# Routing from un-normalised x1 in a decoder layer with a sparse expert stage

## What is computed

```python
h  = rms_norm(x, norm1_g) * (1.0 + scale1) + shift1        # shift, scale, gate from silu(c) @ w_ada
x1 = x + gate1 * mixer(h, ...)                             # conv branch, differential attention, w_o
h2 = rms_norm(x1, norm2_g) * (1.0 + scale2) + shift2
logits = h2 @ w_router + b_router                          # 32 experts
top_vals, top_idx = top_k(logits, 4); wts = softmax(top_vals)
combine = sum(one_hot(top_idx) * wts[..., None], axis=1)
for e in range(32):
    gu  = h2 @ w_up[e] + b_up[e]                           # 1024 -> 2048
    glu = minimum(gu[:, 0::2], 7); lin = clip(gu[:, 1::2], -7, 7)
    act = glu * sigmoid(1.702 * glu) * (lin + 1.0)
    y  += combine[:, e:e+1] * (act @ w_down[e] + b_down[e])
out = x1 + gate2 * y
```

## Time and profile before

| | us |
|---|---|
| median of 3 runs | 1326.64 (1326.07 to 1327.2) |
| profiled execution, whole | 1327.75 |
| its span, first to last instruction | 1326.0 |
| PE busy | 1132.5 (85%) |
| DVE busy | 377.9 (28%) |
| ACT busy | 231.6 (17%) |
| POOL busy | 57.3 (4%) |
| DMA, mean over the span | 360 GB/s |
| mean granted TensorE clock | 0.934 of full |

### The profile page before, as it was taken

The page is one execution under the profiler, slowest core; times in us unless marked ns, Lnnn a source line. Parts: engine busy times, 40 slices in busy tenths (PEclk is TensorE's granted clock), DMA queues, the critical chain, the costliest instruction groups (busy, mean ns, idle before and its releaser), DMA issues.

```text
span 1326.0 us, 18358 instructions
## 1 busy us (share of the span) xinstructions
PE 1132.5 (85%) x7535; PEld 435.1 (33%) x7535; DVE 377.9 (28%) x1043; ACT 231.6 (17%) x448; POOL 57.3 (4%) x76
## 2 busy tenths in 40 slices
PE   3899999999979866667999776987869796999996
PEld 1684345444443211112333221322213231333331
DVE  1599946651251111100222110211101120212221
ACT  1200104450112011000122111111101121111220
POOL 2120000037000000000000000000000000000000
PEclk8899999999989788888999878998889898999998
DMA  8969393266579999999999999999999999599997
GB/s 315 332 237 379 127 378 129 92 175 224 200 267 387 424 426 428 426 425 426 426 424 424 425 426 426 424 426 426 425 425 424 426 427 426 235 409 423 421 425 316
DMA packets 69254, 477.57 MB, mean 360 GB/s; under 512 B 6744, under 2 KB 14969, under 8 KB 33358
## 3 DMA queue, kind: packets, MB, share of 16 engines
q1 hardware_dynamic: 66716, 472.66, 87.2%
q0 software_dynamic: 1200, 3.28, 1.0%
q10 hardware_dynamic: 1282, 0.80, 0.2%
HBM read 473.58 MB, written 1.05 MB: 358 GB/s over the span
## 4 chain that ended last, share of the span: by engine, by line
PE 47%; DMA 23%; SPq 18%; DVE 8%; ACT 3%; issue 1%; DVEq 0%
DMA weights<-in_w_down 18%; SPq L430 16%; PE bank L1372 15%; PE bank L1131 8%; PE bank L1399 8%; DVE weights L809 6%; PE bank L1347 4%; DMA weights<-in_w_up 3%; PE bank L1207 2%; PE bank L1266 2%; PE bank L1334 2%; PE bank L1354 1%; PE bank L1121 1%; PE bank L1340 1%; SPq L399 1%; DMA weights<-in_w_in 1%
## 5 line engine op out<-in xcount | busy, mean ns | idle before, releaser
L1372 PE MATMUL bank<-weights,buf_d 128*32 128x512 f32 x3008 | 393.6, 669 | 132.1 <-DMA weights<-in_w_up 132.1
L1372 PEld LDWEIGHTS bank<-weights,buf_d 128*32 128x32 f32 x3008 | 97.3, 117 | 404.1 <-DMA weights<-in_w_up 200.9
L1399 PE MATMUL bank<-weights,buf_d 128*32 128x512 f32 x1504 | 174.5, 597 | 10.0 <-DMA weights<-in_w_down 10.0
L1059 DVE TENSOR_SCALAR u_conv<-bank 128x256 f32<-128x256 f32 x47 | 20.0, 425 | 460.9 <-PE bank L1372 460.9
L690 ACT ACTIVATE u_conv<-u_conv 128x256 f32<-128x256 f32 x47 | 19.6, 416 | 642.6 <-DVE u_conv L1059 642.6
L1347 PE MATMUL bank<-buf_d 64*128 64x512 f32 x384 | 99.6, 638 | 0.9 <-DVE buf_d L1069 0.9
L809 DVE SCALAR_TENSOR_TENSOR weights<-u_conv,weights 128x256 f32<-128x256 f32 x240 | 99.3, 490 | 0.3
L1069 DVE TENSOR_TENSOR buf_d<-bank,u_conv 128x512 f32<-128x512 f32 x47 | 32.5, 692 | 224.9 <-PE bank L1399 224.9
L1131 PE MATMUL bank<-weights,buf_d 128*128 128x512 f32 x192 | 84.9, 604 | 2.3 <-DVE buf_c L842 2.3
L1399 PEld LDWEIGHTS bank<-weights,buf_d 128*32 128x32 f32 x1504 | 42.5, 109 | 106.7 <-issue 81.4
L1334 PE MATMUL bank<-buf_c,u_conv 128*32 128x256 f32 x768 | 60.4, 387 | 1.1 <-DVE u_conv L1028 1.1
(11 more groups left out here) (261 smaller groups left out, 764.3 us busy)
## 6 DMA issues: line engine op xcount, KB each, us to landing
weights<-in_w_up SPq DMA_DIRECT2D x128, 2048.0 KB, 33.7
weights<-in_w_down SPq DMA_DIRECT2D x64, 2048.0 KB, 37.2
weights<-in_w_ada SPq DMA_DIRECT2D x12, 2048.0 KB, 17.2
weights<-in_w_in SPq DMA_DIRECT2D x10, 2048.0 KB, 12.1
weights<-in_w_in SPq DMA_DIRECT2D x8, 1024.0 KB, 11.8
weights<-in_w_conv_out SPq DMA_DIRECT2D x2, 2048.0 KB, 11.7
weights<-in_w_attn_out SPq DMA_DIRECT2D x2, 2048.0 KB, 8.7
weights<-in_w_o SPq DMA_DIRECT2D x2, 2048.0 KB, 11.1
```

Of the source, the lines that this page charges most:

```text
L1372: ins = t.matmul(UP[SLOTS * g:SLOTS * g + SLOTS, :], xgT[:, r, SLOTS * j:SLOTS * j + SLOTS], w[:, r, NB * g:NB * g + NB], start=False, sto ...
L1399: ins = t.matmul(DOWN[rows, :], actT[:, r, at:at + SLOTS], w[:, g, r, NB * i:NB * i + NB], start=(r == 1 and h == 0 and g == 0), stop=(h = ...
```

## The change

- **Router.** h2 is not made for all tokens any more. The un-normalised x1 is transposed; the router's rows are multiplied beforehand by (1 + scale2) * norm2_g (`wr`), and shift2's part is summed into one row `b2`. The logits come out transposed in four partition groups, are folded by `esum`, and multiplied by each token's 1/rms (`rstd2`) in one step with b2. Both tiles go through top-k together.
- **mod2.** The modulation of the second norm is held as columns: two new PSUM uses ("mod2T") on PE behind the V projection. The 16 POOL transfers that spread modulation rows become 12, for gate1 and gate2.
- **First unit.** All tokens of expert 0's first unit are found from expert 0's rank alone (`pos0`), gathered and transposed before the unit table exists. `routed`, `upper`, `tri`, ranks and the table's base are bf16.
- **Gather.** Units gather raw x1 with rstd2 in `pick`. After the transposition DVE applies scale and shift per column (`apply_mod`). ACT's copy of 512 columns becomes one of 256 (Cmb). pickw's transposes go to bank TR, ahead of act's.
- **Slots.** x_tok has its own buffer. SLOT_ORDER is new; SP's waits on the gate copies and the h2 transposes go, a wait on POOL's bias rows (`ebias_ready`) ahead of chunk 3 is new. POOL starts these rows when the last head's scores are done, with buffers in HEAD_SLOT.
- **Start.** The small loads (lambda, q/k gains, positions; gate and conv-out biases, router, b_ada rows) move from SP's queue to ACT's: eight behind the h1T activations, twelve behind the third GLU sigmoid. The rope and lambda work on DVE moves from ahead of glu_tile(0) to behind glu_tile(2), with ACT's Sin and Exp behind the third sigmoid. The conv taps are loaded as 248 rows of 128 and transposed in two steps.

The diff, cut to its core:

```diff
-GATE_SLOT, VALUE_SLOT, HEAD_SLOT, X_SLOT, SMALL_SLOT = 6, 7, 8, 9, 10
-SLOT_ORDER = (0, VALUE_SLOT, 1, 2, 3, GATE_SLOT, 4, 5, HEAD_SLOT, X_SLOT, SMALL_SLOT)
+GATE_SLOT, VALUE_SLOT, HEAD_SLOT, CONV_SLOT, SMALL_SLOT = 6, 7, 8, 9, 10
+SLOT_ORDER = (0, VALUE_SLOT, 1, HEAD_SLOT, 2, 3, CONV_SLOT, GATE_SLOT, 4, 5, SMALL_SLOT)
...
-        order += [("h2T", 0), ("h2T", 1), ("logits", 0), ("h2T", 2), ("h2T", 3), ("logits", 1)]
-        order += [(name, 0) for name in ("totals", "counts", "ends", "routing", "units")]
+        order += [("x1T", i) for i in range(4)]
+        order += [(name, 0) for name in ("lgT", "logits", "rank", "gather", "ends", "combT", "units")]
...
@@ SP: block loads @@
-                if n == CONV0:
-                    for i, w in enumerate((lambda_q1, lambda_k1, lambda_q2, lambda_k2)):
-                        sp.dma_start(lam_in[:, i, :], w.to_broadcast([P, HD])).then_inc(in_small, 16)
...
@@ SP: expert chunks @@
             load_chunk(0, 2)
+            sp.wait_ge(ebias_ready, 3 * PARTS)
+            load_chunk(0, 3)
             for i in range(2):
                 sp.wait_ge(*used[AOUT0 + i])
-                load_chunk(0, 3 + i)
+                load_chunk(0, 4 + i)
+            full(sp, YA_USE + 3)
+            load_chunk(1, 0)
             full(sp, MT_USE + 3)
-            load_chunk(0, 5)
+            load_chunk(1, 1)
             for i in range(2):
                 sp.wait_ge(*used[WO0 + i])
-                load_chunk(1, i)
-            sp.wait_ge(gate2_ready, 2)
-            load_chunk(1, 2)
-            full(sp, H2T_USE[3])
-            load_chunk(1, 3)
+                load_chunk(1, 2 + i)
             sp.wait_ge(units_ready, 2)
             load_chunk(1, 4)
...
@@ ACT: behind h1T @@
+            for i, w in enumerate((lambda_q1, lambda_k1, lambda_q2, lambda_k2)):
+                load(lam_in[:, i, :], w.to_broadcast([P, HD]), in_small)
...
+            for k in range(3):
+                glu_gate(k)
+            for q in range(3):
+                load(bias_f[32 * q:32 * q + 4, :], b_gate[0].rearrange("(i n) -> i n", n=NB), in_rowsb)
...
@@ ACT: routing @@
+            for i in range(3):
+                square(i // 2, i % 2)
+            for i in range(3):
+                keep_x1T(i)
+            square(1, 1)
+            act_e.wait_ge(h_rms, 1)
+            act_e.wait_ge(h_sq, 4)
+            for tt in range(TT):
+                s.activation(rstd2[:, tt:tt + 1], h_ss[:, 1, tt:tt + 1], ACT.Sqrt, scale=1.0 / D,
+                             bias=h_bias[:, tt:tt + 1]).then_inc(h_rms, 1)
+            full(act_e, LGT_USE)
+            s.copy(lgT_sb, bank(LGT_USE)[:, 0:T]).then_inc(bank_free[LGT_USE % 4], 1)
...
@@ ACT: unit loop @@
                 s.copy(actT, TR[:, 0:T].rearrange("p (r s) -> p r s", r=2)).then_inc(actT_ready, 1)
-                act_e.wait_ge(xt_done, u + 2)
-                s.copy(area_q[:, 0:2 * T], GX[:, :]).then_inc(xc_ready, 1)
+                s.copy(Cmb, TR[:, T:2 * T]).then_inc(cmb_ready, 1)
...
@@ DVE: x1 @@
+            def add_branch(tt, half):
...
+                step(v.tensor_tensor(bank(use)[:, :], bank(use)[:, :], gate1[:, cs], ALU.mult))
+                v.tensor_tensor(x_tok[:, tt, cs], x_tok[:, tt, cs], bank(use)[:, :], ALU.add).then_inc(bank_free[use % 4], 1)
...
@@ DVE: routing @@
+            v.tensor_scalar(pos0[:], bank(RK_USE)[:, T + 4:T + 4 + TT], -ROUTED, None, ALU.add).then_inc(pos0_ready, 1)
+            step(v.tensor_copy(ecol[0:EXPERTS, 0:1], bank(RK_USE)[0:EXPERTS, T:T + 1]))
+            dve.wait_ge(pos0_ready, 1)
+            for tt in range(TT):
+                ins = v.tensor_scalar(pick[:, tt, :], place_s[:, 0, :], pos0[:, tt:tt + 1], rstd2[:, tt:tt + 1],
+                                      ALU.is_equal, ALU.mult)
+            ins.then_inc(pick_ready, 1)
...
+            step(v.tensor_scalar(above[:], thr[:], ecol[e, 0:1], None, ALU.is_lt))
+            step(v.tensor_reduce(ecol[e, 1:2], above[:], axis=AX, op=ALU.add))
+            v.tensor_copy(m_col[:, 0:1], ecol[e, 1:2]).then_inc(m_ready, 1)
...
+            def apply_mod(link, at, done):
+                seen = GX[:, T:2 * T].rearrange("p (r g s) -> p r g s", r=2, g=GROUPS)
+                to = xgT.rearrange("p r (g s) -> p r g s", g=GROUPS)
+                link(v.tensor_tensor(to, seen, xg_scale.unsqueeze(3).to_broadcast([P, 2, GROUPS, SLOTS]), ALU.mult), at)
+                v.tensor_tensor(to, to, xg_shift.unsqueeze(3).to_broadcast([P, 2, GROUPS, SLOTS]), ALU.add).then_inc(done, 1)
...
@@ PE: unit @@
                 gather()
+                pe.wait_ge(pickw_ready, u + 1)
+                for tt in range(TT):
+                    t.transpose(TR[:, T + P * tt:T + P * tt + P], pickw[:, tt, :], ident[:])
                 pe.wait_ge(act_ready, u + 1)
                 transpose_halves(TR, 0, act).then_inc(t_done, 1)
                 pe.wait_ge(xs_ready, u + 2)
-                transpose_halves(GX, T, xg)
-                pe.wait_ge(pickw_ready, u + 1)
-                for tt in range(TT):
-                    ins = t.transpose(GX[:, P * tt:P * tt + P], pickw[:, tt, :], ident[:])
-                ins.then_inc(xt_done, 1)
+                transpose_halves(GX, T, xg).then_inc(xt_done, 1)
```

More of the change, by code:

```diff
@@ L340, in build @@
         WO_USE = use_of["w_o", 0]
-        H2T_USE = [use_of["h2T", i] for i in range(4)]
-        LG_USE = [use_of["logits", i] for i in range(TT)]
-        RT_USE = use_of["routing", 0]
-        TOT_USE = use_of["totals", 0]
-        CNT_USE = use_of["counts", 0]
-        END_USE = use_of["ends", 0]
-        UN_USE = use_of["units", 0]
+        M2T_USE = [use_of["mod2T", i] for i in range(2)]
+        X1T_USE = [use_of["x1T", i] for i in range(4)]
+        LGT_USE, LG_USE, RK_USE, GA_USE, END_USE, CT_USE, UN_USE = (
+            use_of[n, 0] for n in ("lgT", "logits", "rank", "gather", "ends", "combT", "units"))
+        assert GA_USE % 4 == 1
         MEAN_USE, VAR_USE = use_of["mean", 0], use_of["var", 0]
@@ L675, in _, with square @@
-            act_e.wait_ge(lg_ready, 1)
-            s.activation(tw[:], topf[:], ACT.Exp).then_inc(tw_ready, 1)
-            full(act_e, RT_USE)
-            s.copy(routedT[:], bank(RT_USE)[0:EXPERTS, 0:T])
-            s.copy(combT[:], bank(RT_USE)[0:EXPERTS, T:2 * T]).then_inc(bank_free[RT_USE % 4], 1)
+            def square(tt, half):
+                freed(act_e, WO_USE + 2 * tt + half)
+                if tt or half:
+                    act_e.wait_ge(h_sq, 2 * tt + half)
+                s.activation(junk, x_tok[:, tt, NB * half:NB * half + NB], ACT.Square,
+                             accum_out=h_ss[:, half, tt:tt + 1]).then_inc(h_sq, 1)
@@ new lines, in _ @@
+            for i in range(3):
+                add_branch(i // 2, i % 2)
+            dve.wait_ge(h_sq, 3)
+            v.tensor_scalar(h_bias[:], h_ss[:, 0, :], 1.0 / D, EPS, ALU.mult, ALU.add).then_inc(h_rms, 1)
+            step(v.tensor_copy(area_k[:, 2128:2128 + KD], mod2[:, 1, :]))
+            step(v.tensor_copy(area_k[:, 2128 + KD:2128 + 2 * KD], mod2[:, 0, :]))
+            add_branch(1, 1)
+            full(dve, X1T_USE[3])
+            v.tensor_copy(x1T[:, 4:8, P:2 * P], bank(X1T_USE[3])[:, :].rearrange("p (k t) -> p k t", k=4)).then_inc(
+                bank_free[X1T_USE[3] % 4], 1)
@@ L1003, in _ @@
+            ins.then_inc(comb_ready, 1)
             full(dve, END_USE)
@@ new lines, in turn_x1, with seed @@
+            def turn_x1(i):
+                use, tt, half = X1T_USE[i], i // 2, i % 2
+                fill(pe, use)
+                for j in range(4):
+                    kk, r = 2 * half + j // 2, j % 2
+                    ins = t.transpose(bank(use)[:, P * j:P * j + P],
+                                      x_tok[:, tt, T * kk:T * kk + T].rearrange("p (c r) -> p r c", r=2)[:, r, :], ident[:])
+                ins.then_inc(bank_full[use % 4], 1)
+            def seed(tt, i):
+                t.matmul(Y[tt][i][:, :], ident[:], x_tok[:, tt, NB * i:NB * i + NB], start=True, stop=True, skip_group_check=True)
@@ new lines, in _ @@
+            for i in range(4):
+                turn_x1(i)
+            seed(0, 0)
+            fill(pe, LGT_USE)
+            for i in range(4):
+                freed(pe, X1T_USE[i])
+            pe.wait_ge(ws_ready, 2)
+            for r in range(2):
+                for g in range(GROUPS):
+                    ins = t.matmul(bank(LGT_USE)[EXPERTS * g:EXPERTS * g + EXPERTS, 0:T], wr[:, 2 * g + r, :], x1T[:, 2 * g + r, :],
+                                   start=(r == 0), stop=(r == 1))
+            ins.then_inc(bank_full[LGT_USE % 4], 1)
@@ L1293, in _ @@
+            seed(1, 0)
+            seed(1, 1)
             pe.wait_ge(routed_ready, 1)
-            fill(pe, TOT_USE)
+            b = bank(RK_USE)
+            for j in range(TT):
+                for tt in range(j + 1):
+                    t.matmul(b[:, T + 4 + j:T + 5 + j], upper[:, tt, P * j:P * j + P], routed[:, tt, 0:1], start=(tt == 0), stop=(tt == j))
```

(1 more changed line is left out.)

500 lines of the change are left out of this document (265 added, 235 removed).

## The result

The changed kernel takes 1314.28 us in the median of four runs (1313.38 to 1315.13), the ratio to the kernel before is 0.9907 (95% interval 0.9887 to 0.9926): 12.4 us faster. The profiled execution took 1313.38, its span is 1311.6 (before 1326.0). L numbers are lines of the changed kernel from here on; in the experiments they are shifted, mostly by a few, in start_as_before by up to 35 (its L868 is L833).

What follows compares the result with a forecast made beforehand. The prediction took a chain of PE and DVE, then routing, then the expert weight stream at DMA rate as the bound. Its terms, -10.9 + 3.5 + 1.7 - 1.2 = -6.9, gave 1319.7 us by the median, range 1314 to 1327.

Steps and rivals of the forecast that it cites:

- the main case: Whole kernel: the summed forecast of 1319.7 us, own range 1317 to 1323, chance 0.56.
- The terms (a) that place the end: Expert weight stream: it starts for good after its first chunk is used, so shifting the first expert matmul shifts the end.
- The routing, forecast -10.9: From last W_o matmul to first expert matmul: 27.1 us before, first expert matmul at 388.8, a gain of 10.9 us.
- The ScalarE drain: ACT's table change in the routing: a possible 1.38 us drain besides the 1.28 us load, left out of the sum.
- The start, forecast -2.2: Before the first conv matmul: small loads on ACT's queue let w_in come sooner, h1T at 38.7 is next late, -2.2 us.
- The rope and lambda block, forecast +6.2: DVE work moved behind glu_tile(2), onto a path without slack: 5.0 us own work plus ACT's answer, +6.2 us.
- the upstream cost is hidden: Rival: POOL's work meets rope instead of the taps, the early half clock costs less; upstream +1.7, 1316.2 us, chance 0.17.
- Upstream together, forecast +5.2: Everything before the routing: start and rope taken as +3.5 us, plus 1.7 for mod2's transposes, a loss of 5.2.
- mod2's columns: PE between V projection and QK's transposes: two uses of four f32 transposes cost +1.7 us (1 to 2).
- Cover for chunks 7 to 9: Weight chunks before the expert stage: they wait for less and are there by 381, which is cover, not gain.
- The unit loop, forecast -1.2: Expert units: pickw's transposes going first save 0.2 us per unit, -1.2 us together (0 to -2).
- The slower rival: Rival at the start: ACT's small-load issues stall and delay sigmoid, taps and rope's Sin; +8, 1335 us, chance 0.12.

Runs made afterwards that it cites:

- start_as_before: Changed kernel with small loads, rope and lambda work, and ACT's Sin and Exp put back at their earlier places, keeping the new conv-taps form: 1314.21 us.
- delay: Changed kernel with six extra 128x512 f32 matmuls on PE between the unit table and the first unit: 1319.23 us.
- chunks_late: Changed kernel with SP holding weight chunks 7 to 9 until the routing logits are on PE: 1319.93 us.
- best1: Changed kernel with rope and lambda between the first two glu_tiles, POOL's bias operations held until seven QK tiles are done, and PE's loop-bound read earlier: 1305.70 us.
- conv_rows_old: Changed kernel with the conv taps again loaded as one transfer of 31 rows of 4 KB and turned by eight transposes: 1319.08 us.
- small_on_sp: Changed kernel with the eight small loads issued again on SP's queue ahead of w_in: 1321.41 us.
- pool_late: Changed kernel with POOL's five bias operations held until QK's second tile is done, behind 142 us: 1311.73 us.
- after_again: The changed kernel run once more without any edit: 1314.34 us.

## Why the prediction was right, and where it was wrong

**How right.** The direction and the size of the routing's gain were right. The total was not: the main case gave itself 1317 to 1323, and 1314.28 lies below it, near the lower end that came from a case held at 0.17. In the profiled executions the change is -14.4 us where -6.9 was forecast, and nearly all of the miss is upstream of the routing. There two things that the sum did not have (the form of the taps' transfer, and a full clock at the start and under QK) met one that it had too low (rope beside POOL). That the result stayed inside the range is in part luck.

**The terms (a) that place the end.** The stream has no slack: delay and chunks_late moved the end by 4.9 and 5.6 us. The wording was loose: what is shifted is the return of the first chunk, and how soon that follows the first matmul depends on the clock under the first unit.

**The routing, forecast -10.9, measured -11.1.** The sum is right and hides two errors. The steps up to the copy of the table were to take 15.5 us from the last W_o matmul and took 14.0. I let ACT end last at the transposed logits, through its table load; in fact the last router matmul ended at 374.7 and ACT's roots at 374.9, so the load of 1.28 costs 0.1 us there. The gather was to run at half clock (1.93) and ran at full (1.07): the granted clock was still 1.00 from 378 to 384, while before the change it was 0.50 from 388 to 400, where the gather stood. Against that, 1.3 us before the first bias rows was in no term: PE reads the loop bound only after the table's copies. With the read put ahead of that wait, PE stands 0.3 us there in best1, so 1.0 of it is gone. The early gather was said to have 1.5 us to spare against the table; it has 0.46, and without it the time is 4.2 us longer in the median, 3.0 of which the trace shows. It is a real part of the gain.

**The ScalarE drain.** The 1.4 us that the prediction set beside its sum are not seen: ACT's operation before the load ends at 373.04, the load stands at 373.12 (1.28 us), and the next ACTIVATE at 374.41, right behind it.

**The start, forecast -2.2, measured -6.6 at the first conv matmul.** The step that failed is that I took the column loads' change of form for nothing, and h1T's 38.7 as given. Two things held the first conv matmul, each of them hiding the other. With only the small loads moved (conv_rows_old) it is at 39.64, near my 38.7; with only the taps' form changed (small_on_sp) at 38.52; with both at 34.40, and with neither (before) at 40.98.

**The rope and lambda block, forecast +6.2, measured +9.2, and POOL.** The 6.2 us stand alone in pool_late. The 3.0 more are POOL's, and the taps got 2.4 us back (11.57 against 13.95 in start_as_before). This is the rival "the upstream cost is hidden" in part: POOL did meet rope, but the meeting is paid on either side. The Trainium skill (SBUF — State Buffer, Who interferes with whom) also says that a tensor_scalar can enter the two-port modes and then shares POOL's port. I had read rope's single-input operations as outside them. The trace bears out the page: L860 and L856, both TENSOR_SCALAR, took 1.02 and 1.01 beside POOL.

**Upstream together, forecast +5.2, measured -2.4 in the traces.** Against start_as_before the changed kernel's loads, rope and POOL sum to +0.1, not +3.5. The taps' new form is what is left of the start: start_as_before has its first conv matmul at 38.48 against 40.98, and its first QK matmul behind the wait at 140.50 against 142.00. QK's next 48 matmuls take 20.87 in place of 22.56 us, because the granted clock was 0.73 and 0.70 from 142 to 148 before and is 1.00 now. That is 1.7 us in these traces that nothing in the change aims at, and why the clock was up stays open. Windows, the kernel before:

```profile
142.00:145.00 3.00, 3.00 (x5) 1.34 (x6) 2.53 (x10) 0.63 (x2) 0.00 (x0) 0.73 0.00 0
145.00:148.00 3.00, 3.00 (x6) 1.26 (x5) 2.90 (x9) 0.15 (x1) 0.00 (x0) 0.70 0.00 0
```

By the medians (-12.4, less the routing's -11.1) only -1.3 is left for everything upstream and the unit loop together, where the sum had +4.0: so the forecast loss did not come, and the size of what came instead is good to a few us only. mod2's columns cost 0.95 (forecast 1.7: the row that I took, 1.91, is of sixteen transposes, and mod2 has eight).

**Cover for chunks 7 to 9: half right.** DMA had nothing left to move from 378 on, so they were in place by then, and they cost nothing. But they stand there because their waits were moved. With the wait on the logits the same chunks cost 5.6 us, so with the shorter routing that edit is a condition of the gain, not an idle one.

**The unit loop, forecast -1.2, measured -0.9.** Units are 0.09 us shorter, not 0.2. The sum took two of them and a little of the stream's slack; the chain has ten in a row ahead of the last transfer (1127 to 1277 before), and ten are 0.9. But after_again lost 2.7 us behind the same point with the same code, so the 0.9 of the total is within what two executions differ by.

**The slower rival** is out here: ACT's eight small loads took 0.36 to 0.47 us each, the twelve 0.27 to 0.5. It was not empty: in conv_rows_old the same eight took 6.7 us together, the last two 2.94, and ACT still had its table loaded (45.97) before the first gate (48.54).

## What to carry to other kernels

Where two loads or chains end near each other ahead of a waiting matmul, undoing one shows nothing of the other: price them one at a time and together. Small work that is moved out of an idle stretch onto the longest engine's path pays back whatever the move gains; look for the wait inside the same stage (here between two gates) before moving it behind the stage. And check every transfer ahead of the weights for its form (number and length of rows), and every register read for the wait it stands behind. Before a position in one trace is given a price, look at how far it moves between traces of the same code: here up to 4 us by 142 us.

## What the runs showed of the hardware that was not expected

- One 124 KB transfer of 31 rows ahead of the weights costs 4.8 us of the total, against three transfers of the same bytes in rows of 512 bytes (conv_rows_old).
- POOL's five bias operations (4.2 us of work) lengthened what DVE did beside them by 2.4 to 3.0 us: the rope block 9.2 for 6.2, the 30 taps 14.94 for 12.1, 29 taps 13.95 for 11.57.
- After a stretch of short PE work the granted clock was 0.52 to 0.63 for the first unit's w_up: 9.56 us for 64 matmuls (8.2 to 9.9 in the other traces), against 7.04 behind 7 us of dense matmuls at the same place (delay).
- Executions of the same code differ by up to 2.7 us in the first 64 conv matmuls (14.06 to 16.80), with the granted clock from 34 to 38 us at 1.00 in some and 0.50 in one.
